# Merging the V projection with the first head's softmax maxima in the shared-K layers of a hybrid MLA/GQA/windowed attention step

## What is computed

```
z = h @ w_in ;  q, k, v, gate = split(z)
s = q @ concat(k_cache, k).T * scale            # + band mask and sink in layer 2
p = softmax(s)                                  # needs the row maximum of s first
o = p @ concat(v_cache, v)
x = x + gt * ((o * silu(gate)) @ w_out)
```

## Time and profile before

| | |
|---|---|
| median of 3 runs | 4364.03 us (4359.85 to 4364.70) |
| the profiled execution's own time | 4366.46 us |
| its span, first to last instruction | 4364.70 us |
| PE busy | 3982.1 us, 91% |
| DVE busy | 2740.2 us, 63% |
| ACT busy | 2399.3 us, 55% |
| POOL busy | 1259.2 us, 29% |
| granted TensorE clock, mean | 0.959 of full speed |

### The profile page before, as it was taken

How to read it: one execution, slowest core, us unless ns; L and a number is a source line. 1 busy time by engine, 2 the same in 40 slices (tenths; PEclk the granted TensorE clock), 3 DMA queues, 4 the chain that set the end, 5 groups by cost and what they waited for, 6 DMA issues and landing times. The chain is left out here.

```text
span 4364.7 us, 58626 instructions
## 1 busy us (share of the span) xinstructions
PE 3982.1 (91%) x20892; PEld 1947.8 (45%) x20892; DVE 2740.2 (63%) x3651; ACT 2399.3 (55%) x3166; POOL 1259.2 (29%) x875
## 2 busy tenths in 40 slices
PE   5997799999999989999999988888999779999998
PEld 1453244444445544444445544444455324444444
DVE  4315477777555738888845528888542447777754
ACT  3325377777634328777833217778332437777761
POOL 1001034434321204444422103333210103444442
PEclk8998799999999989999999989999999879999999
DMA  4124522322202332222111432332111361221211
GB/s 195 49 79 132 161 62 65 76 62 65 73 14 65 116 101 56 62 65 57 45 61 51 123 107 64 83 82 54 57 43 64 110 188 37 55 48 42 54 34 62
DMA packets 375904, 329.39 MB, mean 75 GB/s; under 512 B 247584, under 2 KB 295264, under 8 KB 374544
## 3 DMA queue, kind: packets, MB, share of 16 engines
q1 hardware_dynamic: 375696, 326.60, 26.8%
HBM read 235.30 MB, written 91.23 MB: 75 GB/s over the span
## 5 line engine op out<-in xcount | busy, mean ns | idle before, releaser
L1506 DVE TENSOR_REDUCE max_parts<-bank 128x1 f32<-128x512 f32 (+2 forms) x1536 | 967.5, 656 | 278.7 <-PE bank L1461 254.6
L726 PE MATMUL bank<-H_hilo,w_hilo 128*128 128x512 f16 (+1 forms) x5832 | 1065.7, 346 | 12.4 <-DVE w_hilo L968 8.1
L1711 ACT ACTIVATE p_f<-bank 128x1024 f32<-128x1024 f32 (+2 forms) x768 | 741.3, 965 | 534.0 <-PE bank L1653 487.4
L1653 PE MATMUL bank<-q_slots,k_slots 96*128 96x512 f16 (+7 forms) x3968 | 937.6, 365 | 0.7 <-ACT p_hi L1715 0.6
L1783 DVE TENSOR_TENSOR p_lo<-p_f,p_hi 128x1024 f16<-128x1024 f32 (+2 forms) x624 | 757.3, 1216 | 162.0 <-ACT p_hi L1715 159.0
L726 PEld LDWEIGHTS bank<-H_hilo,w_hilo 128*128 128x128 f16 x5832 | 572.7, 98 | 504.1 <-issue 16.2
L1715 ACT ACTIVATE p_hi<-bank 128x1024 f16<-128x1024 f32 (+2 forms) x768 | 738.3, 961 | 0.0
L1461 PE MATMUL bank<-k_slots,q_slots 96*128 96x512 f16 (+4 forms) x1536 | 542.0, 382 | 111.4 <-DVE max_parts L1506 62.7
L1624 PE MATMUL bank<-p_hi,v_hi_ones 128*128 128x512 f16 (+2 forms) x1568 | 565.3, 362 | 31.1 <-DVE p_lo L1783 18.6
L1626 PE MATMUL bank<-p_hi,v_lo_zeros 128*128 128x512 f16 (+2 forms) x1568 | 565.6, 361 | 0.0
L1628 PE MATMUL bank<-p_lo,v_hi_ones 128*128 128x512 f16 (+2 forms) x1568 | 564.3, 361 | 0.0
(11 more groups left out here) (173 smaller groups left out, 3620.2 us busy)
## 6 DMA issues: line engine op xcount, KB each, us to landing
ada_w<-in_w_ada SPq DMA_DIRECT2D x48, 768.0 KB, 5.7
gate<-z_ring SPq DMA_DIRECT2D x32, 640.0 KB, 2.9
gate_rows<-gate SPq DMA_DIRECT2D x64, 320.0 KB, 4.0
q_slots<-q_mla SPq DMA_DIRECT2D x64, 240.0 KB, 3.2
k_mla<-hilo_out SPq DMA_DIRECT2D x64, 224.0 KB
k_slots<-k_mla SPq DMA_DIRECT2D x64, 224.0 KB, 4.3
v_hi_ones<-v_scratch SPq DMA_DIRECT2D x64, 224.0 KB, 2.9
v_lo_zeros<-v_scratch SPq DMA_DIRECT2D x64, 224.0 KB, 3.5
```

Of the source, the lines that this page charges most:

```text
L726: ins = pe.matmul(dst, lhs(a, k), rhs(b, k), start=(k == 0 and n == 0), stop=(k == nk - 1 and n == 2))
L1506: dve.tensor_reduce(mx[:, par, t, c:c + 1], MB[(b * NE + k) % 2][:, 0:n], AX.X, ALU.max).then_inc(s_red.h, 1)
L1653: ins = pe.matmul(dst, lhs, rhs, start=(m == 0), stop=(m == len(ops) - 1), skip_group_check=swa)
L1711: act.activation(p32[:, p % 2, 0:cols], src, ACT.Exp, scale=scale).then_inc(s_p32.h, 1)
```

## The change

- In layers 1 and 2 the `values` block is called from inside `attention`, after the buffers for V and the maxima are laid out, and takes the first head's entries with it. Entry k of head 0 is put behind V tile 2 + (4k // 7): two entries each behind tiles 2, 3, 4, 6, 7, 8, one behind tiles 5 and 9, so 14 of them between or right behind the tiles, and the rest (16 in layer 1, 8 in layer 2) after the last tile. PE emits, DVE takes and ACT copies them in their own lists at these places. The attention block begins with the first step.
- V of head 0 is loaded (`load_v`) at the end of SP's list in the `values` block, behind the wait for all V stores; the wait for the store of the new context V comes after it.
- The cached V tiles are done before new tile 5 on ACT and DVE (`cached_hi`, `cached_lo`) rather than after the last; the store batches are tiles 4 to 8, 0 to 3, 9 to 13.
- `load_q` of head 1 moves from the attention block to the `values` block, behind `load_q` of head 0.
- POOL's memsets of `V`, `VL` and (layer 2) the sink rows move to the `values` block, behind its memset of the K row. In layer 2 ACT's table load and its wait for the three memsets, and DVE's `sink_raw`, stand at the head of their lists there.
- PE's loop over V tiles is written out, in the MLA layers too, which otherwise keep their order.

```diff
-        batches = [slice(0, 5), slice(5, 10), slice(10, NKT)] if kind == 0 else [slice(4, 9), slice(9, NKT), slice(0, 4)]
+        EARLY = 5
+        def after_cached(n):
+            return n + 1 + (first_kt if n >= EARLY else 0)
+        batches = ([(slice(0, 5), 5), (slice(5, 10), 10), (slice(10, NKT), NKT)] if kind == 0 else
+                   [(slice(4, 9), after_cached(4)), (slice(0, 4), EARLY + first_kt), (slice(9, NKT), NKT)])
+        entries_after = [[] for _ in range(made + 1)]
+        if pro:
+            for k in range(pro["n"]):
+                at_tile = 2 + k * 4 // 7
+                entries_after[min(at_tile, made)].append(k)
...
@@ SP, values block @@
+                    self.load_q(sp, Q, 1)
...
+                sp.wait_ge(s_st.h, s_st.base + 32 * len(batches))
+                if pro:
+                    pro["load_v"](sp)
+                if new_v is not None:
                     sp.wait_ge(s_new.h, s_new.base + 16)
-                sp.wait_ge(s_st.h, s_st.base + 32 * len(batches))
@@ ACT, values block @@
+                if pro:
+                    pro["act_first"](act)
...
                 for n in range(made):
+                    if first_kt and n == EARLY:
+                        cached_hi()
                     act.wait_ge(s_z.h, s_z.base + n + 1)
...
+                    for k in entries_after[n]:
+                        pro["copy"](act, k)
+                for k in entries_after[made]:
+                    pro["copy"](act, k)
@@ DVE, values block @@
+                if pro:
+                    pro["dve_first"](dve)
...
+                    if first_kt and n == EARLY:
+                        cached_lo()
-                    dve.wait_ge(s_vh.h, s_vh.base + n + 1)
+                    dve.wait_ge(s_vh.h, s_vh.base + after_cached(n))
...
+                    for k in entries_after[n]:
+                        pro["take"](dve, k)
+                for k in entries_after[made]:
+                    pro["take"](dve, k)
@@ POOL, values block @@
                 pool.memset(K[row:row + 1, :, 1, :], MAX_UNIT).then_inc(s_row.h, 1)
+                if pro:
+                    pool.wait_ge(s_row.h, s_row.base + 1)
+                    pro["pool_first"](pool)
@@ PE, values block @@
-                peeled(pe, made // 2, body)
+                for n in range(made):
+                    if above_zero(n - 1):
+                        pe.wait_ge(s_vl.h, s_vl.base + after_cached(n - 2))
+                    for h0, hn in halves:
+                        ins = self.three(pe, psum(n % 2)[:, h0:h0 + hn], lambda s, k: lhs(s, k, n),
+                                         lambda s, k: wv[:, h0 // P:(h0 + hn) // P, s, k, :], KT)
+                    ins.then_inc(s_z.h, 1)
+                    for k in entries_after[n]:
+                        pro["emit"](pe, k)
+                for k in entries_after[made]:
+                    pro["emit"](pe, k)
@@ attention, ahead of its block @@
+        def values_first(pool):
+            pool.memset(V[:, :, :, HD:P], 1.0).then_inc(s_row.h, 1)
+            pool.memset(VL[:, :, :, HD:P], 0.0).then_inc(s_row.h, 1)
+            if swa:
+                pool.memset(erow[:], 0.0).then_inc(s_row.h, 1)
+        def rows_first(act):
+            if swa:
+                act.preload_act_table_set(ORDER_SET)
+                act.wait_ge(s_row.h, s_row.base + 3)
+        if make_values:
+            make_values(dict(n=NE, load_v=lambda sp: load_v(sp, 0, 0, 0), emit=emit_first,
+                             take=lambda dve, k: take_entry(dve, 0, 0, k), copy=lambda act, k: copy_rows(act, 0, 0, k),
+                             pool_first=values_first, dve_first=sinks_first, act_first=rows_first))
@@ attention, its block: SP @@
-                load_v(sp, 0, 0, 0)
+                if not make_values:
+                    load_v(sp, 0, 0, 0)
                 load_gate(sp, 0, 0)
                 load_ada(sp, 0, 0)
-                if not mla:
-                    self.load_q(sp, Q, 1)
                 self.next_load(sp, nx)
@@ attention, its block: PE (and in the same way ACT, DVE, POOL) @@
-                wait_head(pe, 0, 0)
-                for k in range(NE):
-                    emit_entry(pe, 0, 0, k)
+                if not make_values:
+                    for k in range(NE):
+                        emit_first(pe, k)
```

More of the change, by code:

```diff
@@ L1131, in _ @@
                     self.load_q(sp, Q, 0)
-                for batch in batches:
-                    sp.wait_ge(s_vl.h, s_vl.base + (batch.stop - first_kt if batch.start >= first_kt else NKT))
+                    self.load_q(sp, Q, 1)
+                for batch, lows in batches:
+                    sp.wait_ge(s_vl.h, s_vl.base + lows)
                     for s in range(2):
@@ L1693, in _ @@
                 act.preload_act_table_set(ORDER_SET)
-                if swa:
-                    act.wait_ge(s_row.h, s_row.base + 3)
-                for k in range(NE):
-                    copy_rows(act, 0, 0, k)
+                if not make_values:
+                    for k in range(NE):
+                        copy_rows(act, 0, 0, k)
                 def body(i, first, last):
@@ L1739, in _ @@
             def _(dve):
-                if swa:
-                    dve.tensor_scalar(sink_raw[:], sink, 1.0 / scale, None, ALU.mult).then_inc(s_raw.h, 1)
-                    dve.wait_ge(s_raw.h, s_raw.base + 1)
-                for k in range(NE):
-                    take_entry(dve, 0, 0, k)
+                if not make_values:
+                    for k in range(NE):
+                        take_entry(dve, 0, 0, k)
                 def normed(i, p):
@@ L1811, in _ @@
                     pool.tensor_copy(sc32[:, :, 0:2], self.sc[:]).then_inc(s_cw.h, 1)
[L1812 to L1815 removed]
+                if not make_values:
+                    values_first(pool)
                 pool.wait_ge(s_row.h, s_row.base + 2 + swa)
@@ L1980, in build, with make_values @@
             Q, K = head_slots()
-            pr.values(KD, KVH * HD, lambda s, k, t: pr.H[:, s, k, tile_cols(t)], 4,
-                      I[f"c_{name}_v"], O[f"new_{name}_v"], kind, Q, K)
-        pr.attention(kind, Q, K, layer + 1 if layer + 1 < DEPTH else None, [I["w_out"][layer * KD + t] for t in range(2)])
+            def make_values(pro):
+                pr.values(KD, KVH * HD, lambda s, k, t: pr.H[:, s, k, tile_cols(t)], 4,
+                          I[f"c_{name}_v"], O[f"new_{name}_v"], kind, Q, K, pro)
+        pr.attention(kind, Q, K, layer + 1 if layer + 1 < DEPTH else None, [I["w_out"][layer * KD + t] for t in range(2)],
+                     make_values if kind else None)
         own.close()
```

71 lines of the change are left out of this document (34 added, 37 removed).

## The result

The changed kernel takes **4341.21 us** (median of 4 runs, 4340.55 to 4342.13) against 4363.49 us (4359.85 to 4364.70) for the kernel before: ratio 0.9948, with a 95% interval of 0.9934 to 0.9962. So it is faster, by half a percent. The forecast was 4340.0 us, 4331 to 4353. The profiled execution took 4342.13 us, against 4366.46 before: 24.3 us less, where the sum had 24.2; the medians differ by 22.3.

A forecast was written before the change was run, and what follows sets the result against it. PE, busy 91% of the span, bounds the kernel where idle or slowed; DVE's reductions pace the maxima. Gains 12.6 + 11.6 = 24.2 us from 4366.46 give 4342.3; the median, 2.4 lower, 4340 us, range 4331 to 4353.

The forecast's parts named there:

- the sum: Layers 1 and 2, V block to first score matmul: gains of 12.6 and 11.6 us, 24.2 us together.
- Part 1, entries: Layer 1: 14 entries between V tiles cost PE 3.4 us, without waiting for reductions; gain 12.6 us.
- The tail: Layer 1, from the last V tile's low part to the last ACT copy: 12.35 us.
- The barrier: Between the merged V block's last work and the first score matmul: 0.6 us.
- Part 2, layer 2: Layer 2: ACT's wait for memsets stops PE 2.1 us, entries cost 3.6 us; gain 11.6 us.
- Part 3, SP: V stores and loads at the V blocks' ends stay hidden; layer 2 closest, 2601.5 against 2602.3 us.
- rival B: V-store landings still set the block's end, 7.6 us more per layer: gain 9.0, 4355 us; chance 0.05.
- Part 4, POOL: Earlier memsets no longer stall the first negated maximum in layers 1 and 2: no stall counted, else 1 to 2.7 us.
- Part 5, MLA layers at 0: Writing out PE's V loop gains nothing; MLA layers change by 0.
- A: Entries between V tiles do not hide, PE and DVE alternate, 9.6 us for 14: gain 12.0, 4352 us; chance 0.12.
- C: V stretches lose PE's full clock, mean about 0.68: 18 us slower, 4382 us; chance 0.05.
- my case: The forecast's own account of layers 1 and 2: gain 24.2 us, 18 to 32 with its unknowns; chance 0.78.

The follow-up runs named there:

- e3: Changed kernel with three entries behind each V tile rather than 1.75: V block to first score matmul 48.70 us (layer 1) and 52.76 (layer 2), 4350.1 us in all.
- e7: Changed kernel with three entries per V tile in layer 1, the third mid-tile: layer 1 V block to first score matmul 41.49 us, 4336.79 us in all.
- second execution: The changed kernel, unchanged, profiled again: V block to first score matmul 45.29 us in layer 1 and 42.03 in layer 2, 4337.63 us in all.
- e2: Changed kernel with ACT's layer 2 wait for POOL's memsets moved to the first use of the sink rows: layer 2 stretch 40.44 us, 4331.6 us in all.
- e5: Changed kernel with the load of V of head 0 back in the attention block: V block to first score matmul 45.19 and 42.20 us, 4335.4 us in all.
- e4: Changed kernel with POOL's two V memsets in layer 1 held until the first reduction, beside the first negated maximum: stretches 44.60 and 43.85 us, 4338.47 us.
- second pair: Both kernels, unchanged, each profiled a second time: 4366.61 us for the kernel before, 4337.63 us for the changed kernel.
- e8: Changed kernel with PE's V loop in layers 0 and 3 a hardware loop again: 4343.36 us; layer 0's first score matmul to layer 1's V block 1032.9 us.

## Why the prediction was right

By its own steps:

- **Part 1, entries.** Right. Tiles 3.05 us apart (3.06 forecast), the last one evicted at 31.8 us into the block (31.3). The 3.9 us over the old 27.9 are a wait for Q of 0.85 us, which I had put at 0 with "at worst 2 us", and 3.05 us for the entries, for which the sum had 3.4. e3 and e7 show why PE did not wait: two buffers and two entries, not the share of DVE's period that I argued from. The argument gave the right number for this packing and would have given a wrong one for three per tile, as my expectation for e3 did.
- **The tail.** 12.35 us forecast from low part to last copy; 1587.85 to 1599.55 is 11.7. So layer 1 is four misses, +0.85, -0.35, -0.65 and the barrier's -0.3, that leave 45.07 us for 45.5.
- **The barrier.** 0.6 us forecast, taken from the end of a landing; 0.3 us measured, behind an engine.
- **Part 2, layer 2.** The pause of PE was forecast at 2.1 us and is 2.44; in the second execution 1.35, because the half clock of tiles 0 and 1 hides more of it. ACT's release 8.46 us into the block (8.4 forecast). What the sum did not have is the half clock of tile 2 behind the pause, 1.7 us, and e2 shows both go when the wait is moved. That the first execution's 43.84 us came so near to 43.4 is luck: 2.0 us too little for pause and clock stand against 0.7 too much for the entries (2.9 for 3.6), 0.6 for the tail (7.1 for 7.7) and 0.3 for the barrier. In the second execution it was 42.03.
- **Part 3, SP.** Right. In layer 2 SP's last issue ends at 2582.69 and ACT's last work at 2585.15, 2.5 us of room rather than 0.8. e5 puts the early load at zero, and e3's layer 2 is a packing in which rival B comes.
- **Part 4, POOL.** Right: 0.17 and 0.23 us in place of 2.07 and 4.16, and e4 brings the stall back by position alone. By the Trainium skill's rule (SBUF — State Buffer, Who interferes with whom) a tensor_scalar in its two-port mode should stall, and the trace agrees: 3.07 us for `sink_raw`, as long as the memset of K beside it, where before it took 0.30 beside a memset of 0.31. Reductions and operations with one SBUF input should not, and the short reduction of 0.15 us beside e4's memset and the low parts of 0.42 us beside e2's (2545.87, beside the memset from 2544.51) agree. The rule did not give the length: in layer 2 before, the stall lasted to the end of the last of three memsets back to back, in layers 0 and 1 to the end of the second of two, in e4 to the end of the first of two, and in layer 3 the negated maximum took 0.18 us, also ending with the first of two.
- **Part 5, MLA layers at 0.** This is the step that was wrong. A written-out loop was put at nothing because its overhead did not show, but -7.3 and +5.8 us stand there (-3.7 and +4.1 in the second pair), and the sum came out right because they nearly cancel, which is luck. e8 shows that the first goes with the loop. What is behind them, as far as it is known, is below.
- **The rivals.** A did not come, and e3 is what it looks like. B did not come, and e3's layer 2 is what it looks like. C did not come: 0.95 and 0.90 in the V stretches where it wanted 0.68. The psum-cycling oscillation of which the Trainium skill tells (TensorE: Matmul & The Clock Gate, A second HAM failure mode: psum-queue depth-cycling) did not show between the tiles of this kernel, nor in e3 with its longer waits at 1.00. One tile at half clock behind a pause of 2.44 us is all there was between the first granting of the full clock and the tail.
- **From the profiled execution to the median.** I took 24.2 us from an execution 2.4 us above the median; the medians differ by 22.3.
- **The chances** do not quite add up: my case, A and half of B are 0.925 for "faster", not 0.88. Nothing in the forecast hangs on it.

## What to carry to other kernels

Work of another stage is hidden beside a stream of matmuls when it is spread so that each piece finds its buffer free at the moment it is issued: count buffers and the consumer's order first and its busy share second, and if one more piece does not fit at a tile's end, try its middle. A wait at the head of an engine's list holds all that is queued behind it, so put it at the first instruction that needs it. Of a merged block, look at which engine ends it last, and how far behind it the next one is.

## What was not expected of the hardware

**A weight load landed late where an instruction fetch ran among its packets.** The first weights of layer 1's projection (L853) are loaded right behind the last work of layer 0. The view of DMA queues in 1 us there, of the kernel before, and then of the kernel after, in the microsecond in which each shows a fetch:

```profile
q1 hardware_dynamic: 25, 0.10, 63.8%
q8 instruction: 1, 0.02, 17.9%
```

```profile
q1 hardware_dynamic: 24, 0.05, 11.7%
q8 instruction: 1, 0.02, 5.8%
```

The numbers are packets, MB and the share of 16 engines. One packet of 16 KB of instructions took 17.9% of 16 us, 2.9 us of one DMA engine, among the weights before, and 0.9 us after, where it came when the weights were nearly done. Before, the end of the load then ran as on one engine that is behind: from 1320.0 to 1322.4 us its packets went one after another, at 6.0% of the 16 engines, about one of them. Which engine the fetch was on the view does not say. The loads landed after 3.1, 6.2 and 7.0 us (min/median/max) before, and after 3.4, 3.6 and 4.4. What PE made of it is in the timelines of PE, before and then after:

```profile
1325.23 5.28 PE L726 MATMUL bank<-H_hilo,w_hilo 128*128 128x512 f16 x12 [4.47 <-DVE w_hilo L968]
```

```profile
1325.22 5.12 PE L726 MATMUL bank<-H_hilo,w_hilo 128*128 128x512 f16 x23 [1.84 <-DVE w_hilo L968]
```

It waited 4.47 us before and 1.84 after, and behind the longer wait, at half the clock, ran 12 matmuls in 5.28 us where it now runs 23 in 5.12. The view by stretches (columns as above), from the weights' issue to the end of these first matmuls, before and then after:

```profile
1315.33:1341.00 25.67, 21.17 (x121) 12.44 (x122) 5.16 (x4) 9.26 (x12) 0.00 (x0) 0.87 0.33 103
1317.95:1338.20 20.25, 18.38 (x120) 11.70 (x121) 5.17 (x4) 9.27 (x12) 0.00 (x0) 1.00 0.39 130
```

So 5.4 of the 7.3 us of this stretch are the longer wait and the half clock behind it. The second pair has waits of 4.20 and 1.82 us and the same 5.1 us (25.32 less 20.23), more than the 3.7 of its whole stretch. The fetch starts 1.2 us behind the weights' issue in both executions of the kernel before, and 4.1 to 4.3 us behind it in all ten of the changed family other than e8, where the first load lands after 3.4 to 3.6 us. At the last weights of layer 3 (L532) it is the other way round: a fetch falls into the loads after, not before, they land after up to 6.7 us (5.4 before), and PE waits 2.10 us for them (0.28 before). In e8 the fetch is gone from these loads (it starts 11.9 us behind the first), and PE waits 1.07 us.

In e8, whose program differs from the changed one in that loop, the fetch came with the weights again, 1.0 us behind their issue and 1.25 us long, and PE waited 2.40 us. The first matmuls ended 22.50 us behind the issue, 2.3 us later than after, and the whole stretch had the length of before, so there 2 to 3 us more came behind these matmuls. So where the fetch falls is shown to go with that loop, and a late landing was seen in the three executions with the fetch among the weights and in no other. That it goes by the code's length, and that the fetch is what delays the load, is argued and not shown. What else differs in e8's stretch stays open, and I did not try padding the program without changing its work, which would tell.

**The clock behind a pause.** Two executions of one kernel paused for the same event, one for 1.35 us and one for 2.44 us; the first went on at 1.00, the second at the half clock for most of one tile. The other seven executions with this pause fall on the same two sides: 1.21 to 1.57 us and on at 1.00, 2.33 to 2.40 us and then the half clock. They also differ in what came before: in those with the shorter pause PE had run tiles 0 and 1 at the half clock for longer. Waits of up to 1.1 us at the tiles left the clock at 1.00 (e3).
